# Filter spectra from products of rounded halves, and the rotary products on GpSimd

## What is computed

```python
def partial_rope(x): ...            # q and k: x*cos + swapped(x)*sin on 16 of 64 columns of a head
def hyena_filter_spectra(L, ...):
    h = sin(f1 * (z @ w1 + b1)); h = sin(f2 * (h @ w2 + b2))
    h = (h @ w3).reshape(L, N_DIRS, HYENA_ORDER, HYENA_WIDTH) * (decay + DECAY_SHIFT)
    taps = concatenate([hf[0] + hb[0], hf[1:], 0, reversed(hb[1:])])
    return rfft(taps)               # one spectrum per length, order and channel
proj = modulate(rmsnorm(x), ...) @ w_in     # q, k, v, the Hyena columns, the gates
attn = windowed_gqa_sink(partial_rope(q), partial_rope(k), v, sink)
hy = hyena_branch(proj_columns, ..., spec, hyena_bias)
```

## Time and profile before

| | us |
|---|---|
| median of three runs | 1113.68 (1112.47 to 1114.11) |
| profiled execution, its time | 1115.09 |
| its span, first to last instruction | 1113.6 |
| TensorE busy | 1091.2 (98%) |
| VectorE busy | 801.9 (72%) |
| ScalarE busy | 454.6 (41%) |
| GpSimd busy | 109.2 (10%) |

### The profile page before, as it was taken

One profiled execution on the slowest core, in us unless ns is written; L12 is line 12 of the kernel. 1 busy time (PEld: TensorE's weight loads), 2 busy tenths in 40 slices (PEclk: granted clock), 3 DMA queues, 4 the chain that ended last, 5 costly groups with the idle time before them and its releaser, 6 DMA issues.

```text
span 1113.6 us, 16637 instructions
## 1 busy us (share of the span) xinstructions
PE 1091.2 (98%) x6304; PEld 1021.9 (92%) x6304; DVE 801.9 (72%) x1334; ACT 454.6 (41%) x792; POOL 109.2 (10%) x132
## 2 busy tenths in 40 slices
PE   6999999999999999999999999999999999999997
PEld 4787698888899999999899999999999999999886
DVE  5877699889388685556455777787978778788534
ACT  5721156665722322423346232253442526157424
POOL 2101210000334332000000000000000000000000
PEclk9999999999999999999999999999999999999998
DMA  9933454443332333743312331143333232222203
GB/s 347 378 100 116 153 189 135 133 132 112 113 131 105 119 104 124 280 148 111 114 57 94 119 127 57 57 152 97 113 100 109 95 104 95 87 76 76 95 19 115
DMA packets 45525, 138.85 MB, mean 125 GB/s; under 512 B 5051, under 2 KB 10635, under 8 KB 44556
## 3 DMA queue, kind: packets, MB, share of 16 engines
q1 hardware_dynamic: 29024, 80.21, 21.8%
q0 software_dynamic: 11376, 44.84, 11.5%
q10 hardware_dynamic: 5052, 12.81, 3.3%
HBM read 121.61 MB, written 15.74 MB: 123 GB/s over the span
## 4 chain that ended last, share of the span: by engine, by line
PE 91%; DVE 4%; DMA 1%; ACT 1%; issue 0%; DVEq 0%; ACTq 0%
PE acc_ps L750 39%; PE wk L1179 16%; PE acc_ps L1198 12%; PE acc_ps L832 12%; PE wk L1054 2%; PE acc_ps L839 1%; PE wk L989 1%; PE wk L978 1%; PE wk L968 1%; PE wk L1020 1%; PE wk L872 1%; PE wk L885 1%; DVE dot_out L1830 1%; PE wk L890 1%; DMA spec<-filt_out 1%; PE wk L880 0%
## 5 line engine op out<-in xcount | busy, mean ns | idle before, releaser
L750 PE MATMUL acc_ps<-act_hilo,w_hi 128*128 128x384 f32 x1504 | 332.2, 342 | 0.7 <-DVE act_hilo L1785 0.4
L750 PEld LDWEIGHTS acc_ps<-act_hilo,w_hi 128*128 128x128 f32 x1504 | 264.4, 188 | 19.5 <-issue 18.3
L750 PE MATMUL acc_ps<-act_hilo,w_lo 128*128 128x384 f32 x752 | 191.9, 336 | 0.0
L750 PEld LDWEIGHTS acc_ps<-act_hilo,w_lo 128*128 128x128 f32 x752 | 136.6, 188 | 0.0
L1198 PE MATMUL acc_ps<-hidden_hilo,act_hilo 128*128 128x384 f32 x768 | 134.7, 335 | 0.2
L1198 PEld LDWEIGHTS acc_ps<-hidden_hilo,act_hilo 128*128 128x128 f32 x768 | 133.2, 188 | 1.1 <-issue 1.0
L1739 DVE TENSOR_TENSOR w_lo<-w_raw,w_hi 128x1024 fp32r<-128x1024 f32 x61 | 76.3, 1251 | 54.9 <-ACT w_hi L1280 54.0
L1280 ACT ACTIVATE w_hi<-w_raw 128x1024 fp32r<-128x1024 f32 x61 | 64.2, 1052 | 44.3 <-PE acc_ps L750 40.9
L2195 DVE SCALAR_TENSOR_TENSOR xT<-acc_ps,modT,xT 128x512 f32<-128x512 f32 (+1 forms) x32 | 19.7, 617 | 59.8 <-PE acc_ps L832 59.6
L1830 DVE CUSTOM_DVE_ANT_0 dot_out<-dot_ring,c_rows,vecT 128x1024 f32<-128x1024 f32 x48 | 61.6, 1283 | 1.0
L2320 DVE SCALAR_TENSOR_TENSOR xT<-acc_ps,modT,xT 128x384 f32<-128x384 f32 (+2 forms) x96 | 40.5, 478 | 28.9 <-PE acc_ps L1198 28.9
(11 more groups left out here) (301 smaller groups left out, 2026.2 us busy)
## 6 DMA issues: line engine op xcount, KB each, us to landing
w_raw<-in_w_pre SPq DMA_DIRECT2D x50, 512.0 KB, 3.6
dot_ring<-in_w_ada_cols POOLq DMA_DIRECT2D x48, 512.0 KB, 3.8
w_raw<-in_w_up SPq DMA_DIRECT2D x32, 512.0 KB, 3.7
w_raw<-in_w_down SPq DMA_DIRECT2D x16, 512.0 KB, 3.5
w_raw<-in_w_down_half SPq DMA_DIRECT2D x32, 256.0 KB, 2.7
spec<-filt_out POOLq DMA_DIRECT2D x12, 512.0 KB, 3.1
gate_spill<-gates_out ACTq DMA_DIRECT2D x16, 384.0 KB, 2.3
hy_spec<-spec SPq DMA_DIRECT2D x12, 512.0 KB, 5.8
```

The costliest lines, as they stand in the source:

```text
L750: mm = pe.matmul(acc_ps[:, slot, 512 * h:512 * h + HALF], w[:, k, :], src[:, x, k, HALF * h:HALF * h + HALF], start=(first and i == 0), st ...
```

## The change

The tables of the spectra (`filt_tab_hilo`, `filt_tab_p_hilo`) come from the host in two halves. The taps go to one of two fp32 tiles `filt_tap`; ScalarE rounds them into `filt_taps_hi` (in its order at the place where it did nothing for a tap unit), VectorE subtracts into `filt_taps_lo`, one tap unit behind the product, the last at the first spectrum. A spectrum is three float32r matmuls in place of one fp32 one. `filt_taps_lo` and `filt_tap` lie where `c_rows` and `dot_ring` do, so their loads are issued behind the last filter output. The short decay is loaded over the long one after unit 11. `rope(j)` has the same three operations on GpSimd: 0 ahead of the units, 1 to 3 behind the bias of units 0, 8 and 18, 4 behind the ring loads. The mask is loaded behind the last output. VectorE waits for one earlier store per half of a long spectrum.

```diff
+ROPE_AFTER = (0, 8, 18)
...
 sync:
+                if t == T_HY + 1:
+                    sp.wait_ge(f_free, len(FU))
+                    sp.dma_start(mask[:], a["t_mask"]).then_inc(ld_rope, 16)
...
 gpsimd:
-            for n in range(3):
-                dot_load(n)
-            pool.wait_ge(ld_filt2, 16 * 5)
+            def rope(j):
+                pool.wait_ge(ld_swap, 64 * (j + 1))
+                pool.tensor_tensor(rt[:], rt[:], sin[:], ALU.mult).then_inc(rope_step, 1)
+                pool.tensor_tensor(qk[:, j, :], qk[:, j, :], cos[:], ALU.mult).then_inc(rope_mul, 1)
+                pool.wait_ge(rope_step, j + 2)
+                pool.wait_ge(rope_mul, j + 1)
+                pool.tensor_tensor(qk[:, j, :], qk[:, j, :], rt[:], ALU.add).then_inc(rope_done, 1)
+
+            pool.wait_ge(ld_filt2, 16 * 4)
+            pool.wait_ge(ld_rope, 16 * 3)
+            rope(0)
             for f, (g, r, kind, pq, kt) in enumerate(FU):
                 if (kind, pq, kt) == (0, 0, 0):
                     pool.wait_ge(f_free, f + 1)
...
+                if f + 1 == tap_end[0, 1]:
+                    pool.wait_ge(f_free, f + 1)
+                    pool.dma_start(dec[:, 0:2], a["t_decay_p"]).then_inc(ld_filt2, 16)
+                if f in ROPE_AFTER:
+                    rope(ROPE_AFTER.index(f) + 1)
+
+            pool.wait_ge(f_free, len(FU))
+            pool.dma_start(cb[:].rearrange("p g n -> p (g n)"), c_d.rearrange("r n -> (r n)").partition_broadcast(P)).then_inc(ld_c, 16)
+            for n in range(3):
+                dot_load(n)
+            rope(4)
...
 tensor, filt_unit:
-                    pe.wait_ge(f_free, tap_end[g, r])
-                    pe.wait_ge(tap_bias, 2 * g + r + 1)
+                    pe.wait_ge(tap_lo, MODS + taps_for(f) + 1)
...
+                    for at, terms in parts:
+                        n = 0
+                        for tab, m in terms:
+                            for x, y in ((0, taps_hi), (0, taps_lo), (1, taps_hi)):
+                                n += 1
+                                mm = pe.matmul(wk[:, c + at:c + at + 512], tab[x], y[:, p, m, :], start=(n == 1), stop=(n == 3 * len(terms)))
...
 scalar, filt_even:
+                if kind == 0:
+                    n = taps_at.index(f)
+                    if (p, q) == (0, 0):
+                        act_e.wait_ge(tap_bias, 2 * g + r + 1)
+                    else:
+                        act_e.wait_ge(f_free, f + 1)
...
+                    act_e.activation(taps_hi[:, e, ms, :].rearrange("p m n -> p (m n)"), tap[:, n % 2], ACT.Copy).then_inc(tap_hi, 1)
+                    return
...
 vector, filt_out (kind 0):
+                    dve.tensor_tensor(tap[:, n % 2], wk[:, fu_col(f):fu_col(f) + 1024],
+                                      dec[:, 2 * q:2 * q + 2, :].rearrange("p m n -> p (m n)"), ALU.mult).then_inc(f_free, 1)
+                    if n % 4:
+                        taps_low(n - 1)
+                    return
+                while lows[0] < len([x for x in taps_at if x < f]):
+                    taps_low(lows[0])
...
-                for x in range(e, specs[0]):
-                    if x >= 2:
-                        dve.wait_ge(f_stored[(x - 2) % 4], 16 * ((x - 2) // 4 + 1))
+                if g == 1:
+                    dve.wait_ge(f_stored[(e - 2) % 4], 16 * ((e - 2) // 4 + 1))
                 if g == 0:
                     dve.wait_ge(f_free, f)
                     for kt, even in enumerate((fE[1][:], fE[0][:])):
+                        if e:
+                            dve.wait_ge(f_stored[(e + kt - 2) % 4], 16 * ((e + kt - 2) // 4 + 1))
...
-                if 2 <= t <= T_V:
-                    rope(t - 1)
```

More of the change, by code:

```diff
@@ L301, in program, with tap_slot, tap_reader, taps_for @@
                 spec_end[g, r] = len(FU)
+        taps_at = [f for f, unit in enumerate(FU) if unit[2] == 0]
+        def tap_slot(f):
+            g, r, _, e, mp = FU[f]
+            m0 = 2 * r if g else 2 * mp
+            return e, slice(m0, m0 + 2)
+        def tap_reader(f):
+            g, r, _, e, mp = FU[f]
+            if (g, r) == (0, 0):
+                return None
+            return FU.index((0, 0, 1, e, mp) if g == 0 else (0, 1, 1, e, r))
+        def taps_for(f):
+            g, r, _, p, q = FU[f]
+            return taps_at.index(FU.index((g, r, 0, p, q if g == 0 else 0)))
         fu_of = [0] * T_FILT + [6] * 4 + [0] * (T_MERGE - T_FILT - 4)
@@ L485, in _ @@
             weights(3)
-            sp.dma_start(mask[:], a["t_mask"]).then_inc(ld_rope, 16)
             sp.wait_ge(n_hi, KD)
@@ L642, in _ @@
                     pool.wait_ge(f_free, f + 1)
-                    tap = taps[0:1, 0, 2 * r if g else 0, :]
-                    pool.tensor_tensor(tap, tap, pairs[0:1, 512 * r:512 * r + 512], ALU.add).then_inc(tap_bias, 1)
+                    first = tap[0:1, taps_at.index(f) % 2, 0:512]
+                    pool.tensor_tensor(first, first, pairs[0:1, 512 * r:512 * r + 512], ALU.add).then_inc(tap_bias, 1)
                 if kind == 1 and (g, kt) != (0, 0):
@@ L849, in filt_mlp, with even_tab, odd_tab, short_tab @@
                 mm.then_inc(fm_ready, 1)
+            def even_tab(p, j):
+                c = 256 * p + P * j
+                return [ftab[:, x, c:c + P] for x in range(2)]
+            def odd_tab(p, j, kt):
+                c = 512 + 512 * p + 256 * j + P * kt
+                return [ftab[:, x, c:c + P] for x in range(2)]
+            def short_tab(p, odd):
+                c = 256 * p + P * odd
+                return [ftab_p[:, x, c:c + P] for x in range(2)]
             def filt_unit(f):
@@ L2139, in _ @@
                     w3_low()
-                    dve.wait_ge(ld_rope, 16 * 4)
-                    rope(0)
-                units = range(fu_first[t + 1], fu_first[t + 1] + (fu_of[t + 1] if t + 1 < T_MERGE else 0))
-                before = 4 if t == 2 else 1
-                for f in units[:before]:
-                    filt_out(f)
-                if 2 <= t <= T_V:
-                    rope(t - 1)
-                for f in units[before:]:
+                for f in range(fu_first[t + 1], fu_first[t + 1] + (fu_of[t + 1] if t + 1 < T_MERGE else 0)):
                     filt_out(f)
@@ L2594, in tables @@
             out["t_filt_p"] = out["t_filt_p"][:, :, 0, :]
+    even = out["t_filt_s"][:, 0::2, :, 0:P].reshape(P, 512)
+    odd = out["t_filt_s"][:, 1::2].reshape(P, 1024)
+    for n, m in (("s", np.concatenate([even, odd], 1)), ("p", out["t_filt_p"].reshape(P, 512))):
+        m = m.astype(f)
+        bits = m.view(np.uint32)
+        high = ((bits + np.uint32(0x7FF) + ((bits >> np.uint32(12)) & np.uint32(1))) & np.uint32(0xFFFFF000)).view(f)
+        out[f"t_filt_{n}"] = np.stack([high, m - high], 1)
     return {k: np.ascontiguousarray(v.astype(f)) for k, v in out.items()}
```

84 lines of the change are left out of this document (39 added, 45 removed).

## The result

| | before | after |
|---|---|---|
| median | 1113.68 (1112.47 to 1114.11) | 1125.38 (1123.91 to 1126.32) |
| ratio | | 1.0106, 95% interval 1.0091 to 1.0121 |
| profiled execution, its time | 1115.09 | 1126.07 |
| its span | 1113.6 | 1124.4 |

A forecast was written before the change was run, and what follows sets the result against it. TensorE, busy 98% of the span, was taken as the bound. Gains of 5.2 and 1.95 us against new waits of 1.0, 1.35, 4.75, 1.0 and 2.2 summed to +3.15, a median of 1116.8 us, range 1110.5 to 1120.

The forecast's parts named there:

- Matmuls, -5.2: Spectra on TensorE: 32 fp32 matmuls (27.7 us) replaced by 96 rounded ones (22.4 us), -5.2 us.
- Pauses that go, -1.95: TensorE's waits ahead of unit 4 (0.30 us) and unit 17 (1.65 us) disappear, -1.95 us.
- Rotary product on GpSimd, 1.75 each: Each 128x768 rotary product on GpSimd takes 1.75 us, between 1.56 and 1.93.
- Collision: GpSimd products and VectorE operations reading two SBUF operands exclude each other; tap subtractions and weight splits meet rotary products.
- Tile 6: TensorE waits 0.5 us at unit 20 and 4.2 at unit 22; together +4.75 us (4.35 to 5.1).
- tile 3: Rotary product 0 holds up a split and later outputs; TensorE waits at units 4 and 5, +1.0 us.
- tile 5: Weight splits queue behind ScalarE's tap rounding; output 12 is late for unit 14, +1.35 us (1.0 to 1.7).
- turn of the values: Store 8 goes out behind rotary 3; output 22 and then the transposes wait, +1.0 us (0.8 to 1.2).
- scores: First scores wait for rotary 4, done at 150 to 151 while tile 7 is out at 148.5: +2.2 us.
- Behind tile 8 TensorE stays the bound and neither gains nor loses: After tile 8 the change was to cost or save nothing on TensorE.
- Rival (c): Loading c rows and ring where needed delays dot 0 to 153: +5.8 us, 1119.5 us, chance 0.15.
- the sign of being wrong: Dots on VectorE starting after 152 us would show the forecast wrong.

The follow-up runs named there:

- Experiment 4: Changed kernel with GpSimd waiting for a rotary step's first product to end before its second: 1121.46 us, 1.0060 to the kernel before.
- Experiment 3: Changed kernel with unread matmuls keeping TensorE at work in its two longest pauses: 1126.93 us, 1.0110 to the kernel before.
- experiment 5: Kernel before with only the c rows and first three ring rows loaded behind the last filter output: 1118.97 us, 1.0044.
- kernel 1: Changed kernel with the rotary products back on VectorE, halves and late loads kept: 1124.67 us, 1.0091 to the kernel before.
- late_loads_only: The kernel of experiment 5: kernel before with only the c rows and ring loads behind the last filter output, 1118.97 us.
- dummy_softmax_first: Changed kernel with unread matmuls in TensorE's two longest pauses, plus the first softmax's reciprocals ahead of the tile's first dot: 1128.36 us, 1.0129.

## Why the prediction was wrong

**Direction and most mechanisms stood. Two steps failed: VectorE's lateness behind tile 8, which was said to cost nothing, and in TensorE's own row the clock, which had no term. At the turn of the probabilities the two rows are late within 0.3 us of each other.** Step by step:
- *Matmuls, -5.2:* right for undisturbed units, -4.0 by TensorE's busy time less clock. Spectra in rounded halves took 1.4 and 2.8 us where the clock was full. The missing 1.2 lies in short stands of up to 0.3 that count as busy, such as one of 0.3 ahead of unit 20, where 0.5 was forecast.
- *Pauses that go, -1.95:* right; the waits ahead of unit 4 for late taps and of unit 17 aren't there. Unit 4 has one of its own, as expected.
- *Rotary product on GpSimd, 1.75 each:* 1.82 to 1.86 alone, within the bounds (the very first took 1.97).
- *Collision:* right in kind. Tile 6 was mis-sized: 5.7 where the worst single wait was put at 4.2, since I let GpSimd's second product queue behind the waiting VectorE, as it did in the earlier trace rows, where the low half was taken up 0.28 us into the first. Experiment 4 shows it. The Trainium skill (SBUF — State Buffer, "SBUF: two separate sides") has it that whichever instruction starts first gets the shared ports for its whole length and the other fully blocks. The rows agree, but the sentence doesn't settle who is next when one of the two already waits. I read it as first come, first served, by which the subtraction taken up at 130.52 goes ahead of the product begun at 131.16; in experiment 4, where it did, the two took 4.52, and here 6.29.
- *New waits, forecast against trace:* tile 3 1.0 and 0.9; tile 5 1.35 and 2.6 (units 12 and 14); tile 6 4.75 and 5.7; turn of the values 1.0 and 0.5; scores 2.2 and 3.2. Together 10.3 and 12.9.
- *Clock:* no term at all, and no reason given. It withheld 5.1 us of work, and with 2.4 more idle time and 1.2 less gained from the matmuls than forecast this makes TensorE's own row 11.8 longer to the third scores, not 3.15. Experiment 3 shows that lifting the clock alone gives nothing in the kernel after, because VectorE's row is as late. Where a wait at the turn is followed by a fall of the clock, that fall costs 1.5; the last section lists which were.
- ***"Behind tile 8 TensorE stays the bound and neither gains nor loses"* failed**, with the sentence on the windows, that what VectorE is late there is made good at a tenth of the time at best. I had the earlier trace rows in hand, VectorE busy 126.2 of 141.5, and took a queue 89% full for one with slack. In the first 50 us of that stretch it has next to none, busy 48.3 of 50, and one row of the kernel before says what that means, which I didn't read. The window, and TensorE, both before, at the first turn of the probabilities:

```profile
148.50:198.50 50.00, 49.66 (x297) 42.60 (x297) 48.34 (x121) 32.20 (x73) 5.29 (x10) 1.00 0.52 171
...
162.94 1.06 PE L978 MATMUL wk<-ident,att_s 128*128 128x128 f32 x8 [0.34 <-DVE att_max L2014]
```

TensorE already waits there, so in this kernel each microsecond by which the dots start later is one on the time. Dots 10.9 us later gave a span 10.8 us longer. The outputs and the split ahead of the dots are late by the waits that I had priced, and on top of them the first dot waited 1.92 for its load.
- *Rival (c)* named the mechanism, loads of the c rows and the ring at the point of use, with a dot at 153 and 15 in 100. By itself it costs 4.9, from 3.0 to 6.8 (experiment 5); in the changed kernel the dot came at 157, past the 152 that I had set as the sign of being wrong.

Where the lateness of the first dot comes from, by kernels (from the spectra's start, before 79.7): the late loads alone +5.8; halves with early loads on VectorE +5.6; both together +11.4 (kernel 1), so the two add; the products on GpSimd alone +0.6, in the kernel after +0.5 beside the late loads, which cover them, and +4.1 where the loads are early. Left open: why the stores of units 20 and 21 took some 4.9 and 6.8 us (138.30 to 143.17, 139.50 to 146.28, where the waiting outputs began) and not 3.1; two weight loads went out beside the first, and no kernel took these away alone.

## What to carry to other kernels

Ask of each engine beside the bound not how full it is on average, but where its row next meets the bound engine and how many tenths of a microsecond TensorE waits there now: a wait of 0.3 us in the trace means that there is next to no slack, and that nearly all of each delay ahead of it is paid. When a change lets two tiles share memory, price the loads that lose their early place first. And when a long wait of the bound engine is forecast, give the clock a term of its own. And read a releaser's name to the end: which softmax, which tile, whose bank.

## What the runs showed of the hardware

- VectorE's operation with two SBUF operands can stay locked out through two GpSimd products that follow each other directly: 6.29 us for two subtractions, 4.18 for a split of 1.22. In these traces that goes by when it is taken up: at 0.38 to 0.42 us into the first product it went ahead of the second, at 0.53 to 1.16 us only behind the second; nothing was measured between. With a semaphore wait between the products the two cases above took 4.52 and 2.39.
- The granted clock can fall while TensorE still stands (0.50 from 136 to 137, ahead of a matmul at 138.06). A pause doesn't always cost clock. At the first turn, waits of 2.33, 2.47, 2.33, 2.32 and 2.54 were followed by a fall (9.0 us to the third scores), waits of 2.47 (late_loads_only) and 2.71 (dummy_softmax_first) by none (7.5).
- Low clock beside another engine's lateness is free: the 5.1 us withheld ahead of the turn were given back, and the time went from 1125.38 to 1126.93, with 1.5 withheld behind the turn.
